# Prompt attention of a hybrid decoder step: scores issued map by map, with the vector and scalar engines' order changed to match

## The reference, cut to what matters

```python
k2 = k.reshape(B, Tk, H_DIFF, 2, QK_HEAD_DIM)          # QK_HEAD_DIM = 64, two maps
s = jnp.einsum('bqhmd,bkhmd->bhmqk', q, k2) * (QK_HEAD_DIM ** -0.5)
s = jnp.where(dist >= 0, s + bias, NEG_INF)
p = jax.nn.softmax(s, axis=-1)
a = p[:, :, 0] - lam * p[:, :, 1]
o = jnp.einsum('bhqk,bkhd->bqhd', a, v)                # then per-head RMSNorm
```

## Time and profile before

| | us |
|---|---|
| median of 3 runs | 1362.29 |
| lowest and highest | 1362.23, 1364.62 |
| the profiled execution, its own time | 1361.42 |
| its span, first to last instruction | 1359.7 |
| mean granted TensorE clock | 0.999 of full speed |

### The profile page before, as it was taken

How to read it: one execution, slowest core, us unless ns; L and a number is a source line. 1 busy time by engine, 2 the same in 40 slices (tenths; PEclk the granted TensorE clock), 3 DMA queues, 4 the chain that set the end, 5 groups by cost and what they waited for, 6 DMA issues and landing times.

```text
span 1359.7 us, 21879 instructions
## 1 busy us (share of the span) xinstructions
PE 1318.5 (97%) x8386; PEld 1189.5 (87%) x8386; DVE 723.1 (53%) x1175; ACT 446.4 (33%) x751; POOL 172.7 (13%) x323
## 2 busy tenths in 40 slices
PE   7999999978879999999999999999999999999998
PEld 6999999955546788998999989898989898989986
DVE  6447633166677664565354454546463645453555
ACT  6321012045566633352232313131323132322332
POOL 2227000022223221200000000000000000000003
PEclk9999999999999999999999999999999999999999
DMA  8676875278794632222010202020111101020117
GB/s 270 194 255 233 271 240 162 73 201 214 185 262 123 209 124 86 79 77 78 16 62 22 71 15 77 15 77 15 62 31 62 31 28 64 15 77 15 47 47 136
DMA packets 115672, 146.97 MB, mean 108 GB/s; under 512 B 8012, under 2 KB 83445, under 8 KB 115605
## 3 DMA queue, kind: packets, MB, share of 16 engines
q1 hardware_dynamic: 107865, 122.30, 30.1%
q10 hardware_dynamic: 6748, 20.24, 4.0%
q0 software_dynamic: 992, 3.54, 1.6%
HBM read 114.06 MB, written 31.47 MB: 107 GB/s over the span
## 4 chain that ended last, share of the span: by engine, by line
PE 90%; DVE 3%; issue 3%; POOL 2%; ACT 1%; DMA 1%; SPq 0%; DVEq 0%; POOLq 0%; ACTq 0%
PE PS L2410 39%; PE PS L2132 17%; PE PS L2475 16%; PE PS L2353 7%; PE PS L2225 2%; PE PS L2490 2%; PE PS L2505 2%; POOL small L1408 1%; PE PS L2285 1%; PE PS L2187 1%; DVE PS L1577 1%; PE PS L2117 1%; PE PS L2344 1%; DMA x_in<-in_x_prompt_dram 1%; PE PS L2213 0%
## 5 line engine op out<-in xcount | busy, mean ns | idle before, releaser
L2410 PE MATMUL PS<-act_lo,wu_hi 128*128 128x364 f32 (+1 forms) x1056 | 346.4, 328 | 0.0
L2410 PE MATMUL PS<-act_hi,wu_lo 128*128 128x364 f32 (+1 forms) x1056 | 346.0, 328 | 0.0
L2410 PE MATMUL PS<-act_hi,wu_hi 128*128 128x364 f32 (+1 forms) x1056 | 345.9, 328 | 0.0
L2410 PEld LDWEIGHTS PS<-act_hi,wu_hi 128*128 128x128 f32 x1056 | 198.5, 188 | 0.5
L2410 PEld LDWEIGHTS PS<-act_lo,wu_hi 128*128 128x128 f32 x1056 | 198.2, 188 | 0.4
L2410 PEld LDWEIGHTS PS<-act_hi,wu_lo 128*128 128x128 f32 x1056 | 198.3, 188 | 0.0
L1892 DVE TENSOR_TENSOR y_acc<-y_acc,PS 128x512 f32<-128x512 f32 x162 | 111.2, 687 | 115.9 <-PE PS L2475 115.9
L2475 PE MATMUL PS<-wd_hi,g_hi 128*128 128x512 f32 x324 | 130.1, 402 | 0.0
L2475 PE MATMUL PS<-wd_lo,g_hi 128*128 128x512 f32 x324 | 128.0, 395 | 0.0
L2475 PE MATMUL PS<-wd_hi,g_lo 128*128 128x512 f32 x288 | 114.0, 396 | 0.0
L1278 ACT CAST g_hi<-conv 128x1088 fp32r<-128x1088 f32 x21 | 23.2, 1105 | 245.6 <-PE PS L2475 189.6
(11 more groups left out here) (289 smaller groups left out, 2324.2 us busy)
## 6 DMA issues: line engine op xcount, KB each, us to landing
wu_raw<-in_w_up_dram SPq DMA_DIRECT2D x44, 512.0 KB, 4.0
k_tok<-in_cache_k_dram SPq DMA_DIRECT2D x64, 256.0 KB, 4.0
keys_t<-k_turned ACTq DMA_DIRECT2D x32, 512.0 KB, 4.2
vpage<-in_cache_v_dram SPq DMA_DIRECT2D x64, 256.0 KB, 4.2
wd_raw<-in_w_down_dram SPq DMA_DIRECT2D x22, 512.0 KB, 5.3
w_raw<-in_w_in_dram SPq DMA_DIRECT2D x20, 512.0 KB, 6.4
kt_mid<-keys_t SPq DMA_DIRECT2D x20, 256.0 KB, 6.2
kt_b<-keys_t SPq DMA_DIRECT2D x20, 256.0 KB, 6.5
```

The lines of the kernel that those rows point to most:

```text
L2410: mm = nc.tensor.matmul(PS[:, 3 * half + c, 0:kept(c)], a[:, half, k, :], b[:, k, KEPT[c]], start=(j == 0), stop=(j == len(parts) - 1))
```

## The change

On PE, `scores` gets its maps in the outer loop, and its wait is for the one exponent that read the same map. For most steps (`first_map_ahead`: all of 2 to 31 but 4, 8, 9, 11, 12, 16, 17, 19 and 20; step 2 is still issued whole) map 0 is issued a step ahead, between `weigh` and `turn`, and map 1 in the step itself. `smp_scores(i)` moves ahead of the scores in three steps of four. On DVE the minimum of map 0 and `out_norm` go ahead of `mix(i-1)`. On ACT `out_square` goes one step sooner, between the two exponents.

```diff
@@ ACT
         for i in range(NSTEP):
-            if i >= 3:
-                out_square(i - 3)
...
             if i >= 1:
                 exponent(i, 0)
+                if 2 <= i < NSTEP - 1:
+                    out_square(i - 2)
                 if i == NSTEP - 1:
                     split_ahead(0, 1)
                 exponent(i, 1)
@@ DVE
         for i in range(NSTEP):
-            if i >= 2 and early(i):
+            if i >= 2:
                 if wide_step(i):
                     far_max(i, 0)
-                    far_max(i, 1)
+                    if early(i):
+                        far_max(i, 1)
+                    if i >= 3:
+                        out_norm(i - 3)
+                    near_max(i, 0)
                 else:
-                    near_max(i, 0)
-            if i == 3:
-                out_norm(i - 3)
+                    if i - 1 not in JOINED:
+                        near_max(i, 0)
+                    if i >= 3:
+                        out_norm(i - 3)
             if i >= 1:
                 mix(i - 1)
...
-            for m in range(2):
+            if i >= 2:
                 if wide_step(i) and not early(i):
-                    far_max(i, m)
-                if i >= 3 and m == 0 and wide_step(i) and not i == 3:
-                    out_norm(i - 3)
-                if i >= 2 and (wide_step(i) or not early(i) or m == 1):
-                    near_max(i, m)
-                if i >= 3 and m == 0 and not wide_step(i) and not i == 3:
-                    out_norm(i - 3)
+                    far_max(i, 1)
+                if i - 1 in JOINED:
+                    near_max(i, 0)
+                near_max(i, 1)
@@ PE
-        def scores(i, only=None):
+        def scores(i, only=None, maps=(0, 1)):
...
-            for j, (c, e) in enumerate(parts):
-                if only is not None and j != only:
-                    continue
-                user = bank_user(i, 1 if second_bank(i) else j)
-                if user >= 0:
-                    pe.wait_ge(prob_ready, 2 * user + 2)
-                for m in range(2):
-                    d = slice(DH * m, DH * m + DH)
+            for m in maps:
+                d = slice(DH * m, DH * m + DH)
+                for j, (c, e) in enumerate(parts):
+                    if only is not None and j != only:
+                        continue
+                    user = bank_user(i, 1 if second_bank(i) else j)
+                    if user >= 0:
+                        pe.wait_ge(prob_ready, 2 * user + m + 1)
                     mm = nc.tensor.matmul(score_cols(i, m)[:, c:e], qT[d, h, qs], kT[d, h, NS + c:NS + e], start=True, stop=True)
                     mm.then_inc(score_ready if e == w else first_ready, 1)
...
+        def samples_first(i):
+
+            return i >= 2 and i % 4 != 0
+
+        def first_map_ahead(i):
+
+            return 2 <= i < NSTEP and i not in PARTED + JOINED and i - 1 not in JOINED and i not in (QB + 3, 2 * QB + 3)
+
         for i in range(NSTEP):
+            if samples_first(i):
+                smp_scores(i)
             if i in PARTED:
                 scores(i, 1)
+            elif first_map_ahead(i) and i >= 3:
+                scores(i, maps=(1,))
             elif i >= 2 and i - 1 not in JOINED:
                 scores(i)
...
-            if i >= 1:
+            if i >= 1 and not samples_first(i):
                 smp_scores(i)
             if i < NSTEP - 1:
                 if i >= 2:
                     weigh(i - 2)
                 if i + 1 in PARTED:
                     scores(i + 1, 0)
+                elif i >= 2 and first_map_ahead(i + 1):
+                    scores(i + 1, maps=(0,))
                 if i >= 1:
                     turn(i - 1)
```

## The result

The changed kernel takes 1374.85 us (median of four runs, 1372.69 to 1375.53) against 1362.97 for the kernel before: ratio 1.0083, 95% interval 1.0071 to 1.0096. The profiled execution took 1375.53, its span 1373.8, 14.1 more than before. The forecast was 1368 (1365 to 1371.5), so the time lies above the forecast's own bounds, near the rival of the new chains (1373): the sign and the place are right, about six of the twelve us are not in its sum.

A forecast was written before the change was run, and what follows sets the result against it. PE was taken to bound the loop: 27.5 us of added score work against 27.2 idle. By heads -0.9 + 0.5 + 0.5 + 5.4 = +5.5 on 1361.42 gave 1366.9; the median, 0.87 above, 1368 (1365 to 1371.5; wider range 1362 to 1378).

The forecast's parts named there:

- the rival of the new chains: Wide steps: exponent(i, 1) behind square and weighing, or map 1's scores behind it, costs 0.3 to 0.5 us each; 1373, chance 0.15.
- The pair of maps (the decisive step): Scores on PE: one map alone takes as long as both together, so issuing maps apart adds 27.5 us of PE work.
- the 6.0 of the sum: Second head: PE work added by issuing maps apart in steps 10, 13, 14 and 15, 6.0 us.
- The rival of independent maps: Scores: maps don't share the array or one runs twice as fast alone, nothing added; -15 to -17 us, 1346, chance 0.09.
- The weight load: Scores, rival: a weight load in the same row half isn't hidden, 0.1 per further load, 9 us; 1377, chance 0.08.
- Waits won: Attention loop: PE's waits for exponents and weigh's for out_norm go; by this alone nearly all PE slack (27.2 us idle) won.
- four kept waits: Second head: PE still waits 1.05 us in step 8, 0.5 at weigh(9), 0.67 in step 12, 0.6 in step 13; 2.8 kept.
- The walk has that exponent done before PE gets there in all wide steps but 5, 13 and 21: turn(i-1), behind scores that wait for exponent(i, 0), has no price except 0.6 us in those three steps.
- covered: Step 25: exponent(i, 1), held by out_square until weigh(i-2) is done, ends at 5.2 us within PE's 6.65 of work; no price.
- The last head: Steps 24 to 31: slack of 3.85 to 4.0 us all goes, but 9.35 of PE work come: +5.4 us.
- moves along: Behind the loop: PE is full to the output projection, which shifts with the loop's end; nothing added to the sum.
- First and other heads: First head -0.9 us (6.2 added, step 8's scores issued 0.9 sooner); second and third heads +0.5 us each.

The follow-up runs named there:

- one half: Kernel before, order untouched, both maps reading partitions 0 to 63 in the 20 steps the change issues map by map: 1374.45 us, ratio 1.0089.
- ACT's order mended: Changed kernel, out_square later in steps 7, 15, 23 and 9, 17, 28, take_out behind the first exponent in 7, 15, 23: 1369.26 us, ratio 1.0052.
- PE's part alone: Changed kernel's PE order with the DVE and ACT orders of the kernel before: 1393.96 us, ratio 1.0261.
- the crossed pairs: Changed kernel with map 1 of step i issued beside map 0 of step i+1, exponent(i, 0) ahead of take_turned(i-2): 1389.41 us, ratio 1.0197.

## Why the prediction was right in its sign, and where it fell short

*The pair of maps (the decisive step): right.* One map costs what both did, 1.91 against 1.92, and one half costs 3.63. PE's work in the second window rose by 6.6 us (42.31 less 35.70, by the run with ACT's order mended) against the 6.0 of the sum. Most of the difference is step 12, which the forecast didn't count among those that pay. It issues its maps one behind the other, but map 1 now has its own wait between them, for the exponent that ends at 338.6, and the same four instructions take 1.19 us (to the next start at 339.49) instead of 0.63. Before and after:

```profile
336.45 0.70 PE L2187 MATMUL PS<-kT,qT 64*128 64x256 f32 x4
```

```profile
338.30 1.12 PE L2189 MATMUL PS<-kT,qT 64*128 64x256 f32 x4
```

The forecast has this half microsecond as a wait of 0.67. That the wait is what parts the pair here follows from the code and these times; no run tests it. The rival of independent maps (1346) falls.

*The weight load: the rival falls.* Four instructions of one map in one row half are as fast as eight in two, so no load shows. The Trainium skill, "TensorE: Matmul & The Clock Gate", says that a weight load overlaps a matmul in flight only when the row group differs; the 1.91 and the 3.63 us don't agree with it.

*Waits won: right.* `out_norm` 10.8 to 1.1. Of the four kept waits, 2.8 us in the second head, two are there as waits: `weigh(9)` 0.56 for the 0.5 forecast, the sample scores 0.71 for 1.05. The third is the apart maps of step 12, and of the fourth (0.6 in step 13) no more than about 0.2 shows.

*"The walk has that exponent done before PE gets there in all wide steps but 5, 13 and 21", and the square between the exponents "covered": these failed.* In steps 7, 15 and 23 `take_out` and the square each hold an exponent until PE's `turn_out` and `weigh` are through. The rival of the new chains named the right mechanism and came nearest with its 1373, but in the wrong steps (13 and 21) and judged it by PE's work per step, not by what PE issues ahead of the operation that ACT waits for. That, with the sample steps 9, 17 and 28, is 5.6 us by the medians (1374.85 to 1369.26) and 4.2 both by the ratios and by the windows of the loop without the clock's share, shown by moving operations on ACT alone.

*The last head: mis-sized by a little.* +5.4 forecast. With ACT's order mended the third window has +7.65, of which I take 0.7 to be the third head's, like the second's: +6.95. (How a loop of overlapped steps divides into heads depends on the cut: from `turn_out` in step 23 to the first output product it is +5.4.) 0.6 is a wait that I had not in the sum:

```profile
456.71 0.47 PE L2369 MATMUL PS<-wo_hi,act_hi 128*128 128x512 f32 x1 [0.88 <-ACT res L1066]
```

The first output product waits 0.88 for the copy of the last turned outputs, 0.31 before; "moves along" was not quite true. The rest, some 0.9, I put to `weigh` and `turn`, which hold PE a little longer when scores stand next to them. In the run with ACT's order mended ten instructions of `weigh` take 1.31 us by the starts (441.36 to 442.67) and four of `turn` 0.58 (443.30 to 443.88); in the kernel before, without a wait in them either, 1.22 (435.54 to 436.76) and 0.53 (436.76 to 437.29). Over the eight steps such differences add up to about 0.7 and 0.4. That is read from rows and not tested by itself.

*First and other heads.* -0.9, +0.5 forecast; -0.7, +0.7 measured with the order mended; +0.4, +2.4 (less the clock's 1.6) in the changed kernel. That the +0.5 came so close is in part luck: 6.0 of work, 2.8 of kept waits and 8.2 of slack stand in the sum, and by the windows it was 6.6 of work, 1.45 of idle left and 7.4 of idle before.

## What to carry to other kernels

Two products on different halves of the array's rows are one product's time only while they are issued side by side and can start together; before taking them apart to shorten a chain, count what every pair then costs on the engine that becomes the bound. When operations change places on an in-order engine, walk each one back to what it waits for and count all that the other engine issues ahead of that: 4 to 5 us here came from a copy and a square of 0.6 and 0.3 us that stood ahead of an exponent or of another copy. And a wait that is removed shows its worth only if nothing later in the same list waits for the same thing: the run that moved the copy gave 0.4 us by the medians, the one that moved the square too gave 2.5 more (0.24 and 0.86 for the second window).

## What the runs showed of the hardware

TensorE's granted clock fell to 0.50 for some us within the attention loop, in several kernels, and the same products then took nearly twice their time. In the profile of the changed kernel:

```profile
363.48 3.26 PE L2227 MATMUL PS<-v_all,at_sb 128*128 128x128 f32 x14
```

Before, these 14 instructions of `weigh` held PE from 360.61 to 362.24, 1.63 us; here 3.05 (the next starts at 366.53). With the eight transposes behind them, 1.22 us for 1.02 in the last head, that makes the 1.6 us taken off above. In the undisturbed kernels such dips are short and come and go between runs of one kernel (mean clock 0.994 to 0.999 in runs of the kernel before, 0.997 to 0.999 in those of the changed one), so single profiles differ by 1 to 3 us for this reason alone. Two orders had a lower mean clock in all their runs: PE's part alone (0.972 to 0.986; 30 us on end in its profile), and the crossed pairs (0.986 to 0.994). The kernel before with both maps in one half had a dip of some 10 us in its profile. Ahead of the long one PE was busy 10.18 of 13.00 us. What makes the clock fall I can't say from these runs: in the kernel before PE is busy 9.99 of 13.50 us (338.50 to 352.00) and the clock stays at 1.00.
